# Eleven more rows of SBUF as landing places for gathered expert rows, in a one-core encoder layer

## What is computed

```
best_s, best_j = lax.top_k(cand_s, PEER_TOPK)
expert = jnp.take_along_axis(cand_i, best_j, axis=-1)
g = jax.nn.softmax(best_s, axis=-1)
u_e = expert_down[expert]
act = jax.nn.gelu(jnp.einsum('chkd,cd->chk', u_e, xc), approximate=False)
v_e = expert_up[expert]
return jnp.einsum('chk,chkd->cd', (g * act).astype(xc.dtype), v_e)
```

## Time and profile before

| | |
|---|---|
| median of 3 runs | 1824.02 us |
| lowest and highest | 1817.2 and 1826.44 us |
| the profiled execution's own time | 1825.07 us |
| its span in the profile | 1823.3 us |
| mean granted TensorE clock | 0.96 of full |

### The profile page before, as it was taken

The page is one execution under the profiler, slowest core; times in us unless marked ns, Lnnn a source line. Parts: engine busy times, 40 slices in busy tenths (PEclk is TensorE's granted clock), DMA queues, the critical chain, the costliest instruction groups (busy, mean ns, idle before and its releaser), DMA issues.

```text
span 1823.3 us, 14455 instructions
## 1 busy us (share of the span) xinstructions
PE 1473.1 (81%) x4072; PEld 684.6 (38%) x4072; DVE 1116.8 (61%) x2733; ACT 438.7 (24%) x1119; POOL 983.7 (54%) x1054
## 2 busy tenths in 40 slices
PE   6999988888988897766987988876787776776775
PEld 4444557534433553222432333422343322222222
DVE  5550367776666766676565667656455674577644
ACT  3111345322221322122222222212122121122111
POOL 1000000666666666666566666666676666667663
PEclk9999999999999999998899999999898999899999
DMA  9965402999999999999899999999999999999996
GB/s 308 380 236 112 162 4 46 338 366 356 371 355 392 407 373 366 368 366 364 310 359 409 378 366 376 373 358 373 376 360 357 374 361 383 372 348 374 374 378 244
DMA packets 190617, 604.97 MB, mean 332 GB/s; under 512 B 30897, under 2 KB 31305, under 8 KB 190379
## 3 DMA queue, kind: packets, MB, share of 16 engines
q0 software_dynamic: 147456, 536.94, 77.6%
q1 hardware_dynamic: 42027, 64.30, 10.5%
q10 hardware_dynamic: 1056, 2.82, 0.5%
HBM read 600.64 MB, written 3.34 MB: 331 GB/s over the span
## 4 chain that ended last, share of the span: by engine, by line
PE 34%; POOL 19%; issue 14%; DMA 13%; DVE 11%; another core or an unknown queue 6%; ACT 1%; SPq 1%; DVEq 0%; POOLq 0%; ACTq 0%
PE pair L939 17%; POOL big L681 14%; PE pair L691 9%; POOL region_v L681 5%; DMA big<-in_expert_up,expert_idx 5%; DMA region_v<-in_expert_up,expert_idx 3%; DVE big L1528 3%; PE pair L753 3%; DMA big<-in_expert_down,expert_idx 2%; DMA region_v<-in_expert_down,expert_idx 2%; PE pair L779 1%; DVE region_v L1528 1%; PE pair L718 1%; SPq L519 1%
## 5 line engine op out<-in xcount | busy, mean ns | idle before, releaser
L939 PE MATMUL pair<-big 128*128 128x512 f32 x1460 | 728.7, 625 | 196.7 <-DMA big<-in_expert_up,expert_idx 93.3
L1528 DVE CUSTOM_DVE_ANT_0 big<-big,pair 128x1024 f32<-128x1024 f32 x363 | 441.2, 1219 | 267.0 <-DMA big<-in_expert_down,expert_idx 176.6
L939 PEld LDWEIGHTS pair<-big 128*128 128x128 f32 x1460 | 267.2, 196 | 576.2 <-issue 550.7
L681 POOL DMA_INDIRECT big<-in_expert_up,expert_idx x365 | 346.2, 949 | 247.7 <-remote 106.8
L681 POOL DMA_INDIRECT big<-in_expert_down,expert_idx x363 | 346.4, 954 | 123.6 <-issue 101.7
L939 PE MATMUL pair<-region_v,big 128*128 128x512 f32 x588 | 296.1, 625 | 78.9 <-DMA region_v<-in_expert_up,expert_idx 35.9
L1528 DVE CUSTOM_DVE_ANT_0 region_v<-region_v,pair 128x1024 f32<-128x1024 f32 x149 | 181.6, 1219 | 109.9 <-DMA region_v<-in_expert_down,expert_idx 75.2
L1163 ACT ACTIVATE big<-ident,big 128x128 f32<-128x128 f32 x512 | 163.5, 390 | 354.6 <-issue 185.4
L939 PEld LDWEIGHTS pair<-region_v,big 128*128 128x128 f32 x588 | 106.5, 196 | 228.2 <-issue 216.7
L681 POOL DMA_INDIRECT region_v<-in_expert_up,expert_idx x147 | 139.3, 947 | 95.4 <-issue 36.4
L681 POOL DMA_INDIRECT region_v<-in_expert_down,expert_idx x149 | 140.6, 944 | 52.1 <-issue 42.1
(11 more groups left out here) (156 smaller groups left out, 1078.1 us busy)
## 6 DMA issues: line engine op xcount, KB each, us to landing
big<-in_w_ada SPq DMA_DIRECT2D x8, 2048.0 KB, 22.3
big<-in_w_in SPq DMA_DIRECT2D x5, 2048.0 KB, 13.1
big<-in_w_ada SPq DMA_DIRECT2D x16, 512.0 KB, 11.9
big<-in_w_query SPq DMA_DIRECT2D x4, 2048.0 KB
big<-in_expert_up,expert_idx POOLq DMA_INDIRECT x365
big<-in_expert_down,expert_idx POOLq DMA_INDIRECT x363
big<-in_w_out SPq DMA_DIRECT2D x2, 2048.0 KB
big<-na_scr SPq DMA_DIRECT2D x24, 128.0 KB, 4.1
```

The lines of the kernel that those rows point to most:

```text
L681: nc.gpsimd.indirect_dma_start(places[place], None, (expert_down if kind == "down" else expert_up)[0], bass.IndirectOffsetOnAxis(expert_id ...
L939: last = nc.tensor.matmul(pair[t % 2][:, s * HALF:(s + 1) * HALF], diag[:, j, :], places[place][:, s * HALF:(s + 1) * HALF], start=(h == 0 ...
L1528: v.tensor_tensor_reduce(out=places[place], in0=places[place], in1=u_cur[:, :], scale=1.0, scalar=0.0, op0=ALU.mult, op1=ALU.add, accum_ou ...
```

## The change

The table `EXTRA_PLACES` names eleven more rows of 1024 numbers that have held something needed earlier, each with the set from which it may take gathers: the gate row of `mods`, the transposed mixture, `u` of tiles 0, 1 and 2, the gain and bias rows of the first layer norm, the residual stream `x_sb` of tiles 0 and 1, and the two rows of transposed `u`. `first_use` makes POOL wait, once for each, for the semaphore of the last reader. Nothing is computed otherwise than before; no instruction is added to PE, DVE, ACT or SP.

```diff
+EXTRA_PLACES = [("gate", 102), ("mix", 104), ("u", 142), ("ln1_g", 188), ("ln1_b", 188), ("u", 206), ("x", 222), ("x", 286),
+                ("u_t", 382), ("u_t", 382), ("u", 398)]
...
-ALL_PLACES = PLACES + 4 * len(LATE_PLACES)
+SLOT_PLACES = PLACES + 4 * len(LATE_PLACES)
+ALL_PLACES = SLOT_PLACES + len(EXTRA_PLACES)
...
+OPEN_FROM = [0] * PLACES + [RELEASED_AT[RELEASED_BY[p]] + PLACE_SETS for p in range(PLACES, SLOT_PLACES)] \
+    + [slot for _, slot in EXTRA_PLACES]
...
-        if not _held[p] and downs >= RELEASED_AT[RELEASED_BY[p]] + PLACE_SETS:
+        if not _held[p] and downs >= OPEN_FROM[p]:
...
+        places += [mods[:, 0, :], mix_t.rearrange("p k s -> p (k s)"), u_sb[:, 0, :], ln1_rows[:, 0, :], ln1_rows[:, 1, :],
+                   u_sb[:, 1, :], x_sb[:, 0, :], x_sb[:, 1, :], u_t_rows[:, 0, :], u_t_rows[:, 1, :], u_sb[:, 2, :]]
...
+            def first_use(place):
+
+                extra = place - SLOT_PLACES
+                if PLACES <= place < SLOT_PLACES:
+                    pool.wait_ge(pe_group, INDEX[RELEASED_BY[place]] + 1)
+                elif extra == 0:
+                    pool.wait_ge(dve_evac, EVAC[INDEX[("out", (TILES - 1, 1))]][1])
+                elif extra == 1:
+                    pool.wait_ge(pe_group, INDEX[("out", (TILES - 1, 1))] + 1)
+                elif extra == 2:
+                    pool.wait_ge(u_copied, 3)
+                elif extra in (3, 4):
+                    pool.wait_ge(u_ready, TILES)
...
```

More of the change, by code:

```diff
@@ L353, in build @@
         v_beside = w_flat[T5_SLOT][:, 3072:4096].rearrange("p (i d) -> p i d", i=2)
+        u_sb = region_h[:, :].rearrange("p (t d) -> p t d", t=TILES)
         places = [w_flat[T5_SLOT][:, i * D:(i + 1) * D] for i in (3, 0, 1, 2)]
@@ L357, in build @@
         places += [w_flat[slot][:, i * D:(i + 1) * D] for slot, _ in LATE_PLACES for i in range(4)]
+        u_t_rows = region_qw[:, 4096:6144].rearrange("p (i d) -> p i d", i=2)
+        places += [mods[:, 0, :], mix_t.rearrange("p k s -> p (k s)"), u_sb[:, 0, :], ln1_rows[:, 0, :], ln1_rows[:, 1, :],
+                   u_sb[:, 1, :], x_sb[:, 0, :], x_sb[:, 1, :], u_t_rows[:, 0, :], u_t_rows[:, 1, :], u_sb[:, 2, :]]
         na_place_sb = mods[0:T5_BUCKETS, 0:2, :].rearrange("p t (e m) -> p (t e) m", m=2 * P)
@@ L360, in build @@
         v_sb = region_v
-        u_sb = region_h[:, :].rearrange("p (t d) -> p t d", t=TILES)
         x_norm = region_v
@@ L647, in _ @@
             head_norms(2)
+            def first_use(place):
[10 more added lines that the diff above has]
+                    pool.wait_ge(u_ready, TILES)
+                elif extra == 5:
+                    pool.wait_ge(u_copied, 4)
+                elif extra in (6, 7):
+                    pool.wait_ge(var2_ready, extra - 5)
+                elif extra in (8, 9):
+                    pool.wait_ge(pe_group, INDEX[("query", (3, 3, 2, 2))] + 1)
+                elif extra == 10:
+                    pool.wait_ge(u_copied, 7)
             def wait_for_place(gather):
@@ L655, in wait_for_place @@
                 if before is None:
-                    if PLACE_OF[gather] >= PLACES:
-                        pool.wait_ge(pe_group, INDEX[RELEASED_BY[PLACE_OF[gather]]] + 1)
+                    first_use(PLACE_OF[gather])
                     return
```

## The result

The changed kernel takes 1872.43 us (1867.69 to 1875.84, 4 runs), the kernel before beside it 1825.23 (1817.2 to 1826.94, 4 runs). The ratio is 1.0261, with a 95% interval from 1.0232 to 1.0291: slower by 2.6%, where 1814 us, 0.5% faster, was forecast, and outside of the range. The execution shown here took 1871.94 us, with a span of 1870.1.

A forecast was written before the change was run, and what follows sets the result against it. The prediction took the DMA as the bound, losing about a tenth to POOL's pauses; 1825.1 - 7 (more room) - 3 (slack stretch) = 1815.1 us, for the median 1814 us, range 1800 to 1834.

The forecast's parts named there:

- POOL runs at most about 15 sets ahead of the dots: Step pricing the eleven added semaphore waits: each is for something that ended 12 sets or more before, so zero cost.
- the new waits: Eleven semaphore waits on POOL, one per new place: zero, or 5.7 us once if `u_ready` came two sets late.
- What bounds the kernel: Retrieval part: bound by the DMA, which loses about a tenth because POOL stops feeding it now and then.
- The pauses as late counts of PE: POOL's pauses before up gathers: read as waits for `up_done`, 9.5 to 21.3 us after the product's end, reason unknown.
- 0.0048 us a gather for each set of room: Rate from the 8- to 20-place windows, applied to gathers 196 to 1020: 13.7 us, half taken, 7 us gained.
- The slack stretch: At 850 to 900 us, 315 GB/s against about 365, a true shortage of places: 3 us gained, of 0 to 6.8.
- The crossed kinds: With an odd number of places, down gathers wait for `up_done` and up gathers for `dot_done`: costed at nothing.
- the rows' location: Where the new rows lie in memory: dots, products and gathers take the same time, so nothing.
- The slower one: Rival, 0.15: longer POOL runs mean longer silence of counts, ACT stops at the sixteenth diagonal, PE idles: 1840 us.
- The first rival: Rival, 0.19: the stock of places isn't what holds POOL; no gain on the pauses, 1821 to 1824 us.
- the fourth case: Rival, 0.04: the pauses end altogether, gathers come at 1.27 us from gather 602 on, 68 us less, 1750 us.
- What the profile was to show: Signs from gather 530: POOL runs of 30 to 36 gathers between pauses, 1.41 to 1.42 us a gather last.

The follow-up runs named there:

- e9: The changed kernel with each gather reading the indices of the head before, so the wrong experts are fetched: 1835.68 us, ratio 1.0058 to the kernel before.
- e17: The changed kernel, 31 places, with the experts of heads 24 to 31 chosen eight dots sooner: 1836.95 us, ratio 1.0079 to the kernel before.
- e16: The changed kernel as it is, run again beside the kernel before: 1876.91 us, ratio 1.0272.
- e7: The kernel before, 20 places, with gathers of 2 KB a row in place of 4 and dots over 512 elements: 1811.51 us, one run.
- e14: The kernel before, 20 places, with experts of heads 24 to 31 chosen eight dots sooner, on a chip where the kernel before takes 1700.05 us: ratio 1.0000.
- e4: The changed kernel with only the first four new places, 24 in all: 1828.15 us, ratio 1.0047 to the kernel before.
- e18: The changed kernel with 24 places and the experts of heads 24 to 31 chosen eight dots sooner: 1826.72 us, ratio 1.0011 to the kernel before.
- e1: The changed kernel with 31 places, where POOL also waits before each gather as the 20-place kernel would: 1832.14 us, ratio 1.0066 to the kernel before.
- e10: The kernel before, 20 places, with the second half of every up product on PE left out: 1845.17 us, one run.
- e13: The changed kernel, 31 places, with the earlier choice for heads 24 to 31, on a chip where the kernel before takes 1700.05 us: ratio 0.9991.
- e11: The kernel before with one 128x1 operation on POOL ahead of each gather, interval 1.355 us for 1.243: 1844.09 us, ratio 1.0108.
- e12: The kernel before with gathers of 64 rows in place of 128, dots and products over 64 partitions: 2423.43 us.

## Why the prediction was wrong

**The step that failed** is "POOL runs at most about 15 sets ahead of the dots", in the part on the new waits, and with it "they cost nothing". I checked each of the eleven new waits against that lead, and none of them shows on POOL. I didn't check the waits that were there already, and so the sum has no term for them. `idx_ready` allows eight sets of lead at the first gather of each head. In the trace of before it shows once, 5.6 us at the very first gather, because 20 places hold POOL near that lead. The code that says so was among what I had read. Cost: eight stops, 2.0 of the 2.6% (e9: 1.0261 to 1.0058; e17 beside e16: 1.0272 to 1.0079).

**What bounds the kernel** was wrong for this chip. "The kernel is bound by the DMA, and the DMA loses about a tenth" fell with e7: half the bytes gave 0.7%. The stretch at 413 GB/s showed rightly that the transfers could do more, but a rate that goes up and down with POOL is no evidence that the rate is the bound. On the chip of e14 the first half of the sentence would have been right.

**The pauses as late counts of PE** was right as far as it went (DVE's and ACT's counts are late too), and "I can't say why" was, too. What follows from it wasn't: 0.0048 us a gather for each set of room. I took the windows with 8, 12, 16 and 20 places for a slope that goes on. The waits are 181.8 us with 20 places and 184.8 with 31 and no stop at heads (e9), so the slope's continuation, priced at 7 us with 0 to 13.7 around it, is nothing; 24 places were 0.5% slower (e4) or the same (e18).

**The slack stretch**, -3 us of 0 to 6.8: 331 GB/s for 315, by the same formula 50 x 16 / 365 = 2.2 us. From 865 to 880 us, where I wrote above 0.9, the DMA share is 0.70, 0.61 before. By gather 602 the gain is gone: it starts at 1200.86 us, before at 1199.98.

**The crossed kinds, the rows' location and the new waits** at zero: e1 bounds all of it at 0.8% by its interval, e18 at 0.3% for the first four places.

**The rivals.** The slower one had the right sign and the right first step, "a longer run of POOL means a longer silence". It put the price at the wrong resource. ACT's wait for `up_done` didn't grow (29.8 + 7.1 us after, 27.8 + 22.0 before), and the sixteen diagonals weren't reached. What was reached first is DVE's choice. PE's clock did fall below 0.9 in the last third (0.82), which I had named as the sign of that rival; but it is 0.83 in e9 as well, without a stop at heads, so that it tells nothing about this rival. The price of 1840, at most 1855 us, was too low too. The first rival, that places aren't what holds POOL, holds for everything but the stops. The rule of the Trainium skill that about 358 GB/s of HBM bind a core ("DMA: Bandwidth & Descriptors", "Where 436 GB/s comes from") is contradicted again, now by the slices of e14 at 406 to 410 GB/s. In the fourth case the sum is off: 68 us less than 1824 is 1756, not 1750; nothing hangs on it.

**What the profile was to show**: runs of 30 to 36 gathers came, but they end at heads, not at places; 1.41 to 1.42 us a gather in the last stretch came with the changed kernel's 31 places only in e9 (354.2 / 249 = 1.422), and with 24 places in e4 and e18 (354.2 / 250 = 1.417), and neither run was faster for it.

## What to carry to other kernels

Before giving a producer more room, list every wait that it has, not only the one that is loosened: the next one (here the indices, eight sets ahead) takes over at its own distance, and it may stand on an engine that lags most just when the producer runs longest. If an engine waits microseconds for a count of its own last instruction, the delay is in the messages; here neither more places (e9) nor a lighter load on the transfers and DVE (e7) or on PE (e10) bought it back. And a slope read off four settings of one kernel is a price only as long as the same wait ends last.

## What the runs showed of the hardware

- Counts can arrive late by microseconds, an engine's own too: DVE waited 4.29 us for the increment of the instruction before it, and stood idle 24.5 us before 32 such steps in e17. On another chip the same program (e13) had 1.1 us there, and no unnamed wait at all; the kernel before takes 1700.05 us on that chip and 1826.2 on that of e17. It isn't a matter of bytes (e7) or of PE's work (e10), pauses took less time when POOL issued its gathers more slowly (e11), and with gathers of 64 rows, 2.01 us each, hardly a late count is left (e12). In the 300 us of attention ahead of the gathers DVE has no such wait in the trace of before. What in the chip does it stays open.
- A 128-row gather costs POOL 0.94 us and 0.30 us until the next can start. One memset of 128x1 in between hardly changes that interval (1.246 us for 1.243), nor do two (1.243), and an operation on two operands of 128x1 costs 0.11 us (1.355).
- Rows of 4 KB came in at 406 to 410 GB/s in all slices of e14 from the eleventh to the last but one (a slice is 42 us) except one at 361, on one core.
